# A decoder trunk on one core: the sample tokens' share of a 31-tap convolution moves from VectorE to GpSimd

## The reference

```
z_a, z_b, z_g, q, z_m = split(x @ w_in + b_in)
u = z_a[..., :512] * sigmoid(z_a[..., 512:])
c_a = causal_depthwise_conv(concat(buf_a, u), w_conv_a, b_conv_a)   # 31 taps, each channel by itself
y_a = silu(layer_norm(c_a)) @ w_a_out
```

## Time and profile before

| | |
|---|---|
| median of three runs | 1944.51 us |
| span of the profiled execution | 1943.7 us |
| PE busy | 1823.2 us, 94% |
| DVE busy | 1455.3 us, 75% |
| ACT busy | 1050.0 us, 54% |
| POOL busy | 135.4 us, 7% |

### The profile page before, as it was taken

The page is one execution under the profiler, slowest core; times in us unless marked ns, Lnnn a source line. Parts: engine busy times, 40 slices in busy tenths (PEclk is TensorE's granted clock), DMA queues, the critical chain, the costliest instruction groups (busy, mean ns, idle before and its releaser), DMA issues. The chain is left out here.

```text
span 1943.7 us, 30275 instructions
## 1 busy us (share of the span) xinstructions
PE 1823.2 (94%) x11505; PEld 1559.2 (80%) x11506; DVE 1455.3 (75%) x2077; ACT 1050.0 (54%) x1188; POOL 135.4 (7%) x159
## 2 busy tenths in 40 slices
PE   7998999899998998999979989999999999999993
PEld 7887899799987988899857757878787888888772
DVE  6998686755536999767665667888888888887666
ACT  4353754444424444474344555676777676765553
POOL 1110000000001010000020001020202020201000
PEclk9999999999999999999979999999999999999997
DMA  7554344254443555444326679999999999995763
GB/s 263 204 222 184 116 147 144 104 173 152 148 145 109 197 198 195 152 142 141 130 101 251 258 259 350 360 352 357 350 357 348 361 349 371 340 376 205 258 238 90
DMA packets 119394, 447.10 MB, mean 230 GB/s; under 512 B 11057, under 2 KB 11185, under 8 KB 118785
## 3 DMA queue, kind: packets, MB, share of 16 engines
q1 hardware_dynamic: 112288, 424.45, 59.1%
q0 software_dynamic: 7008, 21.34, 3.4%
HBM read 435.68 MB, written 12.67 MB: 231 GB/s over the span
## 5 line engine op out<-in xcount | busy, mean ns | idle before, releaser
L645 DVE TENSOR_TENSOR wpl<-e_ring,wph 128x2048 fp32r<-128x2048 f32 x269 | 607.2, 2290 | 98.4 <-ACT wph L639 97.5
L639 ACT CAST wph<-e_ring 128x2048 fp32r<-128x2048 f32 x269 | 502.2, 1904 | 140.1 <-DMA e_ring<-experts 71.5
L589 DVE TENSOR_TENSOR wl<-ring,wh 128x1024 fp32r<-128x1024 f32 x234 | 285.0, 1222 | 199.5 <-ACT wh L583 198.9
L1773 PE MATMUL psum<-xTh,wh 128*128 128x320 f32 x1184 | 376.1, 318 | 37.8 <-DVE wl L589 21.3
L1774 PE MATMUL psum<-xTl,wh 128*128 128x320 f32 x1184 | 370.7, 313 | 0.0
L1775 PE MATMUL psum<-xTh,wl 128*128 128x320 f32 x1184 | 370.4, 313 | 0.0
L583 ACT CAST wh<-ring 128x1024 fp32r<-128x1024 f32 x234 | 243.6, 1046 | 157.6 <-PE psum L1794 71.2
L2039 PE MATMUL psum<-wph,xe 128*128 128x512 f32 (+1 forms) x768 | 298.0, 388 | 14.8 <-issue 12.0
L2040 PE MATMUL psum<-wph,xe 128*128 128x512 f32 (+1 forms) x768 | 292.0, 380 | 0.0
L2041 PE MATMUL psum<-wpl,xe 128*128 128x512 f32 (+1 forms) x768 | 291.3, 379 | 0.0
L1773 PEld LDWEIGHTS psum<-xTh,wh 128*128 128x128 f32 x1184 | 226.5, 191 | 50.7 <-DVE wl L589 30.6
(11 more groups left out here) (319 smaller groups left out, 2272.3 us busy)
## 6 DMA issues: line engine op xcount, KB each, us to landing
e_ring<-experts SPq DMA_DIRECT2D x264, 1024.0 KB, 6.1
ring<-stream SPq DMA_DIRECT2D x274, 512.0 KB, 3.2
lnp<-rows POOLq DMA_DIRECT2D x4, 1024.0 KB, 6.0
x<-x POOLq DMA_DIRECT2D x3, 512.0 KB, 6.1
arena<-x0T SPq DMA_DIRECT2D x2, 640.0 KB, 6.1
o_a<-arena POOLq DMA_DIRECT2D x2, 540.0 KB, 7.6
o_k<-arena POOLq DMA_DIRECT2D x2, 512.0 KB, 6.5
o_v<-arena POOLq DMA_DIRECT2D x2, 512.0 KB, 8.2
```

The source lines that it names most:

```text
L589: dve.tensor_tensor(wl[:, q % SPLITS, :], ring[:, u % SLOTS, :], wh[:, q % SPLITS, :].bitcast(F32), ALU.subtract).then_inc(lo_done, 1)
L639: act.copy(wph[:, SLOT_OF[m % NPOS], :], ring_place(m).rearrange("p u c -> p (u c)")).then_inc(hi_e, 1)
L645: dve.tensor_tensor(wpl[:, s, :], ring_place(m).rearrange("p u c -> p (u c)"), wph[:, s, :].bitcast(F32), ALU.subtract).then_inc(lo_e, 1)
L1773: pe.matmul(out, h[:, k], hi[:, k], start=(k == 0), stop=False)
```

## The change

For each block, GpSimd now multiplies all 31 taps of all 64 sample positions in one instruction: `windows_a(j)` is a view of `ua` in which the 31 windows overlap, and the tap weights are spread over the 64 positions. The 31x64 products go into `taps_of`, which is the first 1984 values of `cb`. Four sums in place then halve them to two parts, a fifth adds these into `ca`, and a last instruction adds the bias. Each waits for the one in front of it by a semaphore. Blocks 0 and 1 stand ahead of the waits for the keys' and values' banks, blocks 2 and 3 behind the transfers of `o_k` and `o_v`, ahead of the tail copies. VectorE keeps the prompt's multiply-adds. It waits for all four blocks (`samples_a`) before `conv_b`, which writes `cb`; so do TensorE before the mean and ScalarE before it overwrites `ua`.

```diff
--- before.py
+++ after.py
@@ -75,6 +75,9 @@
 MEAN_AFTER = 4
 TAIL, HEAD = T, T + NSAMP
 LAST = 3
+TAPS_A = K_A - 1
+SUMS_A = [(0, 16, 15), (0, 8, 8), (0, 4, 4), (0, 2, 2)]
+STEPS_A = 2 + len(SUMS_A)
 SCORES = [0, 1, 2, 3, 8, 4, 5, 6, 7, 9]
 BRANCHES = [(2, "yc"), (0, "ya"), (1, "yb")]
 SEG_A = K_A - 1 + DSEQ
...
@@ -389,7 +392,9 @@
         sg = blocks_of(v, JA, T)
         v, sah = share(JA * T, ("sah", JA, T))
         ca = blocks_of(v, JA, T)
-        cb = cut(JB * T, JB)
+        cb_flat = cut(JB * T)
+        cb = blocks_of(cb_flat, JB, T)
+        taps_of = cb_flat[:, 0:K_A * NSAMP]
         v, oTl = share(JC * T, ("oTl", JC, T))
         qT, part = blocks_of(v, JC, T), blocks_of(v, 2, T)
         v = cut(DEC * P + H_C * N_MEM + 2 * D_C)
...
@@ -613,6 +619,11 @@
         def seg_a(j, k, n):
 
             return ua[:, j, K_A - 1 + SEQ:LEN_A].rearrange("p (b s) -> p b s", b=DEC)[:, :, k:k + n]
+
+        def windows_a(j):
+
+            seg = seg_a(j, 0, DSEQ)
+            return bass.AP(tensor=seg.tensor, offset=seg.offset, ap=[seg.ap[0], [1, K_A], seg.ap[1], [1, DSEQ]])
 
         def seg_b(j, k, n):
             return zb[:, j, K_B - 1 + SEQ:LEN_B].rearrange("p (b s) -> p b s", b=DEC)[:, :, k:k + n]
...
@@ -795,6 +806,28 @@
                     pool.wait_ge(x_ready, LN_STEPS * 2 * l)
                 pool.dma_start(lnp[:], rows[l, 0:2].partition_broadcast(P)).then_inc(ln_in, 16)
 
+                def samples_of(j):
+
+                    at = STEPS_A * (JA * l + j)
+                    taps = col(l, "w_conv_a", K_A * j, K_A).unsqueeze(2).unsqueeze(3)
+                    if j:
+                        pool.wait_ge(samples_a, JA * l + j)
+                    pool.tensor_tensor(taps_of.rearrange("p (k b t) -> p k b t", k=K_A, b=DEC), windows_a(j),
+                                       taps.to_broadcast([P, K_A, DEC, DSEQ]), ALU.mult).then_inc(samples_step, 1)
+                    part = lambda k, n: taps_of[:, NSAMP * k:NSAMP * (k + n)]
+                    for m, (a, b, n) in enumerate(SUMS_A):
+                        pool.wait_ge(samples_step, at + m + 1)
+                        pool.tensor_tensor(part(a, n), part(a, n), part(b, n), ALU.add).then_inc(samples_step, 1)
+                    pool.wait_ge(samples_step, at + STEPS_A - 1)
+                    pool.tensor_tensor(ca[:, j, SEQ:T], part(0, 1), part(1, 1), ALU.add).then_inc(samples_step, 1)
+                    pool.wait_ge(samples_step, at + STEPS_A)
+                    pool.tensor_scalar(ca[:, j, SEQ:T], ca[:, j, SEQ:T], col(l, "b_conv_a", j), None, ALU.add)\
+                        .then_inc(samples_a, 1)
+
+                pool.wait_ge(glu_done, 2 * JA * (l + 1))
+                pool.wait_ge(hist_ready, HIST * (l + 1))
+                for j in range(2):
+                    samples_of(j)
                 for n in range(H_C):
                     emptied(pool, l, "k", n)
                 for n in range(2):
...
@@ -804,8 +837,8 @@
                         pool.dma_start(x[:, t, :], x0[r0:r0 + P]).then_inc(x_in, 16)
                 pool.dma_start(o_k[l], kT).then_inc(kv_out, 16)
                 pool.dma_start(o_v[l], vm).then_inc(kv_out, 16)
-                pool.wait_ge(glu_done, 2 * JA * (l + 1))
-                pool.wait_ge(hist_ready, (l + 1) * HIST)
+                for j in range(2, JA):
+                    samples_of(j)
                 for j in range(JA):
                     pool.tensor_copy(tail_a[:, j, 0, :], ua[:, j, SEQ:SEQ + K_A - 1]).then_inc(tails_ready, 1)
                     pool.tensor_copy(tail_a[:, j, 1:9, :], seg_a(j, DSEQ, K_A - 1)).then_inc(tails_ready, 1)
...
@@ -1041,7 +1074,8 @@
                     made(l, "rg", n)
                     frees(act.activation(rr[:, n], bank(l, "rg", n)[:, 0:T], ACT.Sigmoid,
                                          bias=col(l, "b_rg_a", n)), l, "rg", n)
-                act.wait_ge(conv_a_tap, K_A * (l + 1))
+                act.wait_ge(conv_a_tap, TAPS_A * (l + 1))
+                act.wait_ge(samples_a, JA * (l + 1))
                 act.wait_ge(tails_ready, 2 * (JA + JB) * (l + 1))
                 for n in range(JB):
                     made(l, "rg", JB + n)
...
@@ -1363,16 +1397,15 @@
                     dve.wait_ge(glu_done, 2 * (JA * l + j + 1))
                     frees(dve.tensor_scalar(ca[:, j, 0:SEQ], ua[:, j, 0:SEQ], col(l, "w_conv_a", K_A * j),
                                             col(l, "b_conv_a", j), ALU.mult, ALU.add), l, "za", 2 * j)
-                    ins = dve.tensor_scalar(samp(ca[:, j, SEQ:T]), seg_a(j, 0, DSEQ), col(l, "w_conv_a", K_A * j),
-                                            col(l, "b_conv_a", j), ALU.mult, ALU.add)
-                ins.then_inc(conv_a_tap, 1)
+                for j in range(JA):
+                    emptied(dve, l, "za", 2 * j)
                 def tap(k):
 
-                    dve.wait_ge(conv_a_tap, K_A * l + k)
+                    if k > 1:
+                        dve.wait_ge(conv_a_tap, TAPS_A * l + k - 1)
                     for j in range(JA):
-                        w = col(l, "w_conv_a", K_A * j + k)
-                        mac(ca[:, j, 0:SEQ], ua[:, j, k:k + SEQ], w, ca[:, j, 0:SEQ])
-                        ins = mac(samp(ca[:, j, SEQ:T]), seg_a(j, k, DSEQ), w, samp(ca[:, j, SEQ:T]))
+                        ins = mac(ca[:, j, 0:SEQ], ua[:, j, k:k + SEQ], col(l, "w_conv_a", K_A * j + k),
+                                  ca[:, j, 0:SEQ])
                     ins.then_inc(conv_a_tap, 1)
 
                 def largest(n):
...
@@ -1416,11 +1449,14 @@
                     split_at(l, "g", 2, n)
                     if n == 3:
                         samples_lo(0)
+                    if n == 0:
+                        dve.wait_ge(samples_a, JA * (l + 1))
                     if n in (0, 1, 2, 6):
                         conv_b({0: 0, 1: 2, 2: 4, 6: 6}[n])
                     if n == MEAN_AFTER + 1:
                         filled(dve, l, "mean", 0)
-                        dve.wait_ge(conv_a_tap, K_A * (l + 1))
+                        dve.wait_ge(conv_a_tap, TAPS_A * (l + 1))
+                        dve.wait_ge(samples_a, JA * (l + 1))
                         frees(mac(ca[:], over(bank(l, "mean", 0)[:, 0:T], JA), -1.0 / D_A, ca[:]), l, "mean", 0)
                         emptied(dve, l, "mean", 0)
                         dve.tensor_tensor(sg[:], ca[:], ca[:], ALU.mult).then_inc(dev_ready, 1)
...
@@ -1918,7 +1954,8 @@
                     elif key[0] == "g":
                         blocks((l, *key), xTh, xTl, T)
                     elif key[0] == "mean":
-                        pe.wait_ge(conv_a_tap, K_A * (l + 1))
+                        pe.wait_ge(conv_a_tap, TAPS_A * (l + 1))
+                        pe.wait_ge(samples_a, JA * (l + 1))
                         take(pe, l, "mean", 0)
                         for j in range(JA):
                             ins = product(bank(l, "mean", 0)[:, 0:T], ones[:], ca[:, j], j, JA)
```

More of the change, by code:

```diff
@@ L516, in trunk @@
         glu_done = sem("glu_done")
+        samples_step, samples_a = sem("samples_step"), sem("samples_a")
         conv_b_done = sem("conv_b_done")
```

## The result

The changed kernel takes 1982.64 us (median of 4 runs, 1979.74 to 1984.04), the kernel before 1943.63 us beside it (4 runs, 1940.37 to 1944.61). The ratio is 1.0199, 95% interval 1.0185 to 1.0213: 39 us slower. The forecast was 1960 us, 16 us slower. The sign was right; the loss is more than twice the forecast.

The account below looks back on a forecast made before the run. VectorE was taken to bound the tap stretch: TensorE 12.6 us later less 5 given back, 7.6 a layer, taken as 8, 16 in both; 1943.7 + 16 + 0.8 = 1960.5, stated as 1960 us, range 1950 to 1972.

Parts of the forecast that it names:

- the direction: Whole kernel: the change makes it slower, 1960 us, 16 us more; slower by over 0.2% given 0.63.
- the sum that GpSimd costs VectorE: Tap stretch of each layer: VectorE loses 32.1 us to GpSimd's new work.
- The samples were never late: Rival at `conv_b`: blocks over 29 us stop VectorE at `samples_a`, end beyond 2000 us; 0.08 together with two passes.
- the wait of 3.34 us: TensorE's wait for VectorE's splits at the gates, before 162.46 us: forecast to be gone, won wholly.
- the first rival: Tap stretch: GpSimd keeps VectorE out for its whole duration, 43 us a layer, 1983 us; chance 0.18 (1972 to 1992).
- their mean from 47 to 110 us: Sign in the taps: the mean of VectorE's 256-value multiply-adds rises from 482 ns by 100 to 200.
- the price: Tap stretch: VectorE stands only while GpSimd fetches, 1.02 ns for each of 31,488 values read a layer.
- netting the gain against the loss: Until GpSimd is done, about 116 us: VectorE gains 16.5 us, loses 32.1; TensorE about 12.6 us later.
- what comes back: Last ten taps give back 7.8 us; TensorE uses 5, including the 3.34 us wait before 162.46.
- A few tenths of clock either way: Each layer: clock changes taken as a few tenths beside the net 7.6 us, which was rounded to 8.

Follow-up runs that it names:

- with the samples left out: Changed kernel without GpSimd's product, sums and bias, zeros written instead: 1883.87 us, total not comparable because the experts have less to multiply.
- the small instructions bunched: Kernel before, with the samples' 124 small VectorE instructions a layer run in 8 bunches of four taps: 1977.58 us.
- the product on VectorE: Kernel before, with each block's samples done on VectorE by one product, one reduce and one bias, GpSimd as before: 1972.14 us.
- the close pieces: Changed kernel with GpSimd's products and its sums of 960 and 512 cut into instructions of up to 256 values: 1960.41 us.
- the same pieces spread: Changed kernel with GpSimd's work in pieces of up to 256 values, its 72 pieces paced evenly over VectorE's 30 taps: 1950.99 us.
- the kernel with both: Kernel before, keeping all VectorE instructions, with GpSimd's blocks added and their results written to scratch: 2003.06 us.

## Why the prediction was wrong

**Right: the direction, and nearly the sum that GpSimd costs VectorE.** 28.8 us a layer against 32.1. The samples were never late, and the wait of 3.34 us went. The sign that was to speak for the first rival came too: the longest multiply-add took 4.5 us, and their mean from 47 to 110 us rose from 484 to 835 ns, not by the 100 to 200 that were forecast.

**Right for the wrong reason: the price.** I took VectorE to stand still only while GpSimd reads: 1.02 ns a value. The rows show the rival's mechanism: VectorE stands for nearly the whole of an instruction (3.83 us beside 3.64). But the rival's sum did not come either. GpSimd's instructions of the four blocks last 41.6 us in layer 0, near its 43 (the product 1.9 ns a value and not 2.7, the small sums more: 64 values in 0.38 us), and VectorE loses 28.8 of them, since by the timelines it gets in work of its own between two of GpSimd's instructions. That 32.1 came near is luck; so is the rival's 1983 us, which is the time measured. The Trainium skill ("SBUF — State Buffer", "Who interferes with whom") says that the first to start holds the shared ports for the whole instruction and that the other fully blocks: by that rule the trace agrees on the blocking, for two-input instructions on both sides (4.5 us here; 1.23 us of a copy beside a split in rows 7 and 8). I had let the one row of L846 (0.83 us lost beside 2.79) stand against it, an instruction of another form.

**The sum, step by step.** By the starts of the same TensorE instructions in both traces:

| step, a layer | forecast | measured in layer 0 |
|---|---|---|
| TensorE's delay behind GpSimd's last block, 116 us of the kernel before | 12.6 | 16.5 |
| behind the wait at the gates, 168 us of the kernel before | 7.6 | 11.3 |
| behind `conv_b`, mark B | 7.6 | 18.3 |

**The first failed step: netting the gain against the loss.** "VectorE has gained 20 x 0.78 + 0.9 = 16.5 us and lost 32.1, net 15.6 more work", less 3 of idle time, 12.6 at TensorE. Measured: 16.5, and 16.2 at mark A. With the 28.8 us that were lost, the same netting would have said 9.3, so the step is 7 us a layer short and the price, too high by 3.3, hid half of that. The netting treats VectorE's time between 46 and 116 us as one account. It isn't: TensorE has at most two split units ahead of it, so a run of VectorE without a split beyond that is lost at once. The lighter taps give back only in part: in the changed kernel TensorE was 10.0 us late at the instruction that stood at 70 us before, and 6.3 at the one that stood at 90, while with the samples left out VectorE only waited longer for ScalarE (23.1 us). Four rows of the table show what one account hides. With the account at zero, the small instructions bunched cost 13.6 us at mark A, and the product on VectorE 11.0. With the account at 21.7 against 24.3 the close pieces cost 6.5 us, and the same pieces spread 1.2. From the changed kernel to the spread pieces mark A moves by 15.0 us (14.2 if the start is set equal), of which the smaller loss (28.8 to 21.4) can explain 7.4; an estimate from these rows is that the lumps, with the clock behind them, make the other 7.

**The second failed step, as large: what comes back.** "The ten taps behind it give back 7.8 us. [...] I take 5." The 5 us did come: from 16.5 late to 11.3, the wait of 3.34 us and the slow clock behind it among them. Then 7.0 us were lost again, a term that the sum doesn't have: `conv_b` stands behind a split whose weights land 16.1 us later, like mark A, so TensorE is 16.1 late again behind its wait of 5.74 us, and 18.3 some 5 us further on, by a lower clock. Windows of the changed kernel and of the kernel before behind this wait:

```profile
199.00:203.00 4.00, 4.00 (x16) 4.00 (x17) 1.95 (x2) 0.00 (x0) 0.00 (x0) 0.50 0.92 326
```

```profile
183.00:187.00 4.00, 4.00 (x27) 3.84 (x26) 1.98 (x2) 1.55 (x3) 0.00 (x0) 1.00 0.94 353
```

With `conv_b` ahead of that split, 2.7 us a layer are had back. Layer 1 repeats the whole loss (18.2 us).

**"A few tenths of clock either way".** In the windows of the taps, the granted clock of 0.87, 0.99 and 0.85 in place of 1.00 makes 26 x 0.13 + 33 x 0.01 + 21 x 0.15 = 6.9 us of full-speed time a layer, an upper bound, since part of it falls on TensorE's waits. Behind the wait of 5.38 us it ran partly at the lower of its two levels; these rows are windows of the changed kernel behind that wait and behind the one of 4.53:

```profile
66.00:76.00 10.00, 10.00 (x71) 10.00 (x71) 10.00 (x19) 2.65 (x4) 1.62 (x4) 0.77 0.51 165
117.60:122.00 4.40, 4.35 (x19) 4.35 (x20) 4.33 (x9) 0.00 (x0) 3.79 (x6) 0.61 0.75 244
```

Over those two, 10 x 0.23 + 4.4 x 0.39 = 4.0 us are lost while TensorE was busy all the time. So an estimate is that 4 to 7 us a layer are clock by mark A, and 2 more behind `conv_b`. The rows around 162.46 in the trace before had shown 0.62 behind a wait of 3.34, and I gave the same mechanism no price where longer waits were to come.

**What stays open.** How much of the changed kernel's 16.2 us is the clock and how much the waits themselves isn't separated in that kernel. The kernel with all in pieces comes near: 6.5 us late with at most 1.7 of clock, so waits cost by themselves. In the kernel with both, the clock was as low as 0.67 from 105 to 126 us, and the delay still equals VectorE's stops: a lower clock seems to cost nothing where TensorE would have waited anyway. Nor was the row of three taps without a split broken up by itself, the edit that would test the longest run alone. That the experts take back 2 us was seen and not explained.

## What to carry to other kernels

VectorE feeds TensorE here through a buffer of two units, and such a producer can't be balanced over a stretch: work moved off it in small even portions and put back in lumps was a loss in each of these runs, even at an equal sum. So price the longest run without a hand-over, and the clock behind the wait that it makes. Look, too, at what stands behind the wait that you hope to win: here it was a transfer that keeps step with the bounding engine. Work for GpSimd beside a full VectorE goes in short instructions, spaced by VectorE's own progress: that made 1951 us of 1983, still 6 more than the kernel before. Before moving anything, ask what the removal would be worth alone; here it was 3 us a layer, against stops of 21 us at best.

## What the runs showed of the hardware

- A one-input instruction of VectorE from and to SBUF was held up too: 3.83 us for 256 values beside a product of 3.64 on GpSimd, 0.41 alone. By its recorded start it even began first, by 0.05 us, so the recorded starts don't say who holds. I had expected such stops of two-input instructions only. The Trainium skill ("SBUF — State Buffer", "Who interferes with whom") counts `tensor_scalar` among those that can contend; the trace agrees.
- In short instructions the two engines take turns: 8 pieces of 256 values took GpSimd 7.38 us, one product of 1984 3.64, while VectorE went on at a little over half its pace (3.16 us for a tap of 1.67).
- On VectorE a product of 1984 values took 2.22 us, the reduce of as many to 64, over a view whose innermost step is 64 values, 3.61.
